# Gated delta rule round: three reorderings around the sixth level of the triangular inverse

## The chip, the cores and the metric

The program runs on one NeuronCore of a Trainium2 chip. The metric is the device time of one execution in microseconds; less is better. The engines are TensorE (PE), VectorE (DVE), ScalarE (ACT), GpSimd (POOL) and SyncE (SP, which here only starts weight loads). Each engine runs its own instruction stream in order and waits on semaphores.

## What is computed

Two blocks run one after the other on a sequence of 1024 tokens of width 1024, all in float32: a hybrid mixer (gated delta rule plus a convolution branch), cross attention over 256 memory rows and a gated feed-forward layer, and then a second block whose modulation is `silu(c) @ w_ada`. The change lies in the stage of the gated delta rule. The reference works in chunks; what matters is the unit triangular solve of each chunk and the recurrence over the chunks:

```
L = where(strict, einsum('id,jd->ij', kb, kc) * decay, 0)
sol = triangular_solve(eye + L, [v*beta, kb*exp(gc)])       # u, w
attn_intra = einsum('id,jd->ij', qc, kc) * decay
def step(S, ...):
    v_new = u_i - w_i @ S
    o = (q_i * exp(g_i)) @ S + a_i @ v_new
    S = S * exp(g_last) + k_dec.T @ v_new
# second block, independent of the first until its end:
mod = silu(c) @ w_ada + b_ada
```

## The kernel before

The sequence is cut into 8 tiles of 128 tokens; a tile holds 4 heads, side by side as 4 blocks of 128 columns. The stage `DeltaRule` is a software pipeline over rounds r = -1 to 9. In round r the engines prepare tile p = r+1 (`prep`), invert the triangle of tile i = r (`inv`) and carry the state for tile o = r-1 (`state`). The order in each round is written out by hand, once for each engine, in the methods `act`, `pe` and `dve`; semaphores (`after`, `prior`) tie them together.

The inverse is built in levels. The next tile's start, level 0, is: TensorE transposes the level-0 block `C0` (`ct`, L1667), VectorE makes `U` from it (`u0`, L1872), masks the level-1 block `C` (`c1`, `level_mask`, L1739) and copies `Tm` compactly to `Tc` (`x1`, `compact`, L1715). These three are "the next tile's triangle" here. Levels 1 to 6 are each: TensorE `y` (L1512, product of `U` and `C`), ScalarE copies it to `Y` (`copy_y`, L1475), TensorE `dd` (L1523, `d`, and up to level 5 also L1527, `t`), VectorE `update` (L1707 for `U`, L1710 for `Tm`, L1715). The sixth level is the last of a round: `y6`, its copy, `dd(i, 6)`, and `u6` on VectorE.

Other work shares the rounds. In even rounds 0 to 6 the convolution branch subtracts a mean (`cent`, L1854), in odd rounds 1 to 7 it makes a variance (`v_m`, L1858), and ScalarE raises it to the power -1/2 (L1440, L1442). GpSimd adds tiles for it in odd rounds (L1226, L1228). The state's output of tile o is scaled on VectorE: a small reduction (L1845 to L1061), ScalarE's `on_ln` and `on_y` (L1433, L1435), five small refinements (L1066 to L1862), the scaling `on` (L1865) and the product with the gate `og` (L1868). Once `og` is done ScalarE starts the load of a later gate into the freed buffer (`load_gate`, L1316), in rounds 1 to 6; instructions behind it on ScalarE wait until then.

The modulation of the second block has 12 weight strips, multiplied one strip at a time by `ada(j)` on TensorE (L1501) into a PSUM bank, from which `keep_ada` on ScalarE copies (L1326). Rounds 0 to 3 have two strips, rounds 4 to 7 one. The second strip of a round is the last item of TensorE's round, and its `keep_ada` stands on ScalarE behind `load_gate`. The next round begins on TensorE with transposes of q, k and v (`rows`, L1552) into the same banks, which wait for all strips kept; then `y1` (L1512), then column sums `ss` (L1562) of the squares `sq` that ScalarE makes as the first item of its round (L1366). VectorE begins its round's `prep` with `ss` (L1758). Then follow the transposes of the output (`oT`, L1574), which wait for the last state update `s3` (L1882), and `wT` (L1580), which waits for `u6`.

"The turn of round r" stands below for the stretch from `ct` of round r to `ss` of round r+1. After round 7 there is no next tile; TensorE goes on with the output product (L294), for which GpSimd splits weights (L3591, L3593).

Of the kernel before, what the change touches and what calls it, by code (L numbers as in the profile page):

```python
# [24 lines left out]
ALU = mybir.AluOpType  # L25
# [104 lines left out]
def after(eng, steps, name, rnd, back=0):  # L130

    eng.wait_ge(steps.sem, steps.at(name, rnd) - back * steps.n)


def prior(eng, steps, name, rnd):

    if rnd >= 0:
        after(eng, steps, name, rnd)


def build(nc, d, out):

    ctx = ExitStack()
    with ctx:
# [3 lines left out]
        def place(name, shape, dt=F32, at=None):  # L148

            at = top if at is None else at  # L150
            size = int(np.prod(shape[1:])) * 4
            t = nc.alloc_sbuf_tensor_at(name, shape, dt, offset=at["at"])
            at["at"] += (size + 63) // 64 * 64
            return t
# [7 lines left out]
        ident = place("ident", [P, P])  # L162
# [37 lines left out]
        def bank(b):  # L200
            return pp[b // 2][:, (b % 2) * 512:(b % 2) * 512 + 512]
# [28 lines left out]
        def mixed(x, l, pair=None):  # L230

            sz, whole = 1 << l, x[:, :, :]
            first, pairs = (0, 2) if pair is None else (pair, 1)
            return bass.AP(whole.tensor, whole.offset + first * P, [list(whole.ap[0]), [2 * sz, pairs * P // (2 * sz)], [2 * P + sz, 2], [1, sz]])

        def natural(x, l):

            return x.rearrange("p h (b two n) -> p (h b) two n", two=2, n=1 << l)
# [72 lines left out]
        class Stage:  # L311
# [25 lines left out]
            def act(self, act):  # L337
                pass
# [29 lines left out]
        class ResidualNorm:  # L368
# [31 lines left out]
            def load(self, act, t):  # L400
                s = t % self.slots
                act.dma_start(self.x[s][:, :], self.src[t * P:(t + 1) * P, :]).then_inc(norm_loaded[s], 16)
# [672 lines left out]
        class DeltaRule(Stage):  # L1075
# [233 lines left out]
            def act(self, act):  # L1309
# [46 lines left out]
                for r in range(-1, NT + 2):  # L1356
                    p, i, o = r + 1, r, r - 1
                    prep, inv, state = p < NT, 0 <= i < NT, 0 <= o < NT
                    f, fq = r % 2, r // 2
# [68 lines left out]
                        keep_ada(j)  # L1428
                    if 0 <= r < len(MEM_STRIPS):
                        self.keep_mem(act, r)  # L1430
                    if state:
                        after(act, self.ov, "on_m", o)
                        O_.done(act.activation(self.s4[:, 6, :], self.s4[:, 5, :], ACT.Ln), "on_ln")  # L1433
                        after(act, O_, "on_ln", o)
                        O_.done(act.activation(self.s4[:, 6, :], self.s4[:, 6, :], ACT.Exp, scale=-0.5), "on_y")  # L1435
                    if o == NT - 1:
                        branch(1, ("hi",))
                    if f == 1 and 0 <= fq < 4:
# [1 line left out]
                        F.done(act.activation(self.cr[1][:, :], self.cr[0][:, :], ACT.Ln), "v_ln")  # L1440
                        after(act, F, "v_ln", fq)
                        F.done(act.activation(self.cr[1][:, :], self.cr[1][:, :], ACT.Exp, scale=-0.5), "v_y")  # L1442
                    if inv:
                        self.copy_y(act, i, 6)
                    if prep and p + 2 < NT:
                        after(act, self.ps, "kq", p)
# [30 lines left out]
            def pe(self, pe):  # L1477
                PP, I, O = self.ps, self.is_, self.os
                def gates(*us):
                    for u in us if p == 0 else ():  # L1480
                        self.src.gate_unit(pe, u)
# [9 lines left out]
                def ada(j):  # L1491
                    strip = FIRST_STRIP[f"ada{j}"]
                    if j:
                        pe.wait_ge(self.ada_kept, j)
                    if prep:
                        after(pe, self.pv, "l3", p)
                    for half in range(2):
                        pe.wait_ge(w_loaded[half], (RAW_AT[strip] // 2 + 1) * 16)
                        for part in range(ADA_PARTS):
                            k = half * ADA_PARTS + part  # L1500
                            last = pe.matmul(bank(self.K_)[part * 32:part * 32 + 32, 0:SC], ada_c[:, k:k + 1].broadcast_to((P, 32)),  # L1501
                                             w_raw[:, k * SC:(k + 1) * SC], start=(half == 0), stop=(half == 1))
                        last.then_inc(w_ready, 1)
# [11 lines left out]
                def dd(i, l):  # L1515
                    after(pe, self.ia, f"y{l}", i)
                    if l == 1:
                        prior(pe, self.iv, "u6", i - 1)
                        after(pe, self.pv, "x1", i)
                    else:  # L1520
                        after(pe, self.iv, f"x{l}", i)
                    for pair in range(2):
                        last = pe.matmul(bank(self.B_)[:, pair * P:(pair + 1) * P], self.Tc[i % 2][:, pair, :], self.Y[:, pair, :], start=True, stop=True)  # L1523
                    I.done(last, f"d{l}")
                    if l < LEVELS - 1:
                        for pair in range(2):
                            last = pe.matmul(bank(self.A_)[:, pair * P:(pair + 1) * P], self.Y[:, pair, :], self.Tc[i % 2][:, pair, :], start=True, stop=True)  # L1527
                        I.done(last, f"t{l}")

                for r in range(-1, NT + 2):  # L1530
                    p, i, o = r + 1, r, r - 1
                    prep, inv, state = p < NT, 0 <= i < NT, 0 <= o < NT
                    f, fq = r % 2, r // 2
                    jobs = list(self.ada_of(r))
# [128 lines left out]
                    if prep:  # L1663
                        after(pe, self.pv, "c0", p)
                        after(pe, self.pa, "egb", p)
                        for pair in range(2):
                            last = pe.transpose(bank(self.G_)[:, pair * P:(pair + 1) * P], self.C0[:, pair, :], ident[:, :])  # L1667
                        PP.done(last, "ct")
                        gates(*range(11, 16))
                    if inv:  # L1670
                        dd(i, 6)
                    for j in jobs[1:]:
                        ada(j)

            def dve(self, dve):
                PV, IV, OV, F = self.pv, self.iv, self.ov, self.fv
                sm, al, tt = self.sm, self.al, dve.tensor_tensor
# [13 lines left out]
                def scal(x):  # L1691
                    return x.rearrange("p (h a) -> p h a", a=1).broadcast_to((P, GH, P))
# [21 lines left out]
                def compact(i, l):  # L1714
                    (IV if l > 1 else PV).done(dve.tensor_copy(natural(self.Tc[i % 2][:, :, :], l), mixed(self.Tm[i % 2], l)), f"x{l}")  # L1715
# [18 lines left out]
                def level_mask(i, l):  # L1734
                    if l > 2:
                        after(dve, self.is_, f"y{l - 2}", i)
                    else:
                        prior(dve, self.is_, f"y{l + 4}", i - 1)
                    (IV if l > 1 else PV).done(tt(self.masked(l, self.C[l % 2][:, :, :]), self.mixed(self.L[i % 2], l), self.masks(l, low_masks[:, l, :]), ALU.mult), f"c{l}")  # L1739

                for r in range(-1, NT + 2):
                    p, i, o = r + 1, r, r - 1
                    prep, inv, state = p < NT, 0 <= i < NT, 0 <= o < NT
                    f, fq = r % 2, r // 2
# [111 lines left out]
                    if f == 1 and 0 <= fq < 4:  # L1856
                        after(dve, self.fs, "sumsq", fq)
                        F.done(dve.tensor_scalar(self.cr[0][:, :], bank(self.F_)[:, 256:512], 1.0 / CW, EPS, ALU.mult, ALU.add), "v_m")  # L1858
                    if state:
                        recip_sqrt_refine(dve, self.oa, OV, "on", o, s4[:, 5, :], s4[:, 6, :], s4[:, 7, :])  # L1860
                        after(dve, OV, "on_r", o)
                        OV.done(tt(s4[:, 6, :], s4[:, 6, :], sc[:, o, RQ, :], ALU.mult), "oy")  # L1862
                        after(dve, OV, "oy", o)
                        prior(dve, self.os, "oT", o - 1)
                        OV.done(tt(self.on[:, :, :], b4(self.O2), scal(s4[:, 6, :]), ALU.mult), "on")  # L1865
                        after(dve, OV, "on", o)
                        skipped = ("s0", "s1", "s2", "s3") if o == NT - 1 else ()
                        OV.done(tt(self.on[:, :, :], self.on[:, :, :], self.gate[o % 2][:, :, :], ALU.mult), "og", *skipped)  # L1868
                    if prep:
                        after(dve, self.ps, "ct", p)  # L1870
                        after(dve, self.pa, "ui", p)
                        PV.done(tt(self.mixed(self.U[p % 2], 0), self.masks(0, ident[:, :]), self.masked(0, self.two(self.G_)), ALU.subtract), "u0")  # L1872
                        level_mask(p, 1)
                        after(dve, PV, "t0", p)
                        prior(dve, self.is_, "d6", p - 2)
                        compact(p, 1)
                    if inv:
                        update(i, 6)
                    if state and o < NT - 1:
# [1872 lines left out]
```

## Time and profile before

| | us |
|---|---|
| median of 3 runs | 2740.36 |
| lowest, highest | 2728.75, 2741.19 |
| the profiled execution | 2739.87 |
| its span | 2737.9 |

In the span TensorE is busy for 2618.3 us (96%), VectorE for 1660.1 us (61%), GpSimd for 1137.8 us (42%) and ScalarE for 835.1 us (31%). The rounds in which the change acts (r = 0 to 7) take from about 324 to 597 us of the span. A row of a timeline gives start, duration, engine, line, operation and tiles, and in brackets the idle time of the engine before it and who ended it. A matmul row that covers several instructions overlaps the next row by a pipeline's length, so starts are compared, not ends.

### The profile page before, as it was taken

To read this page: it belongs to the slowest core of one execution; us is meant where nothing else is said; L and a number is where in the kernel's file an instruction comes from. 1 tells how busy PE (TensorE), PEld (TensorE's weight loads), DVE (VectorE), ACT (ScalarE), POOL (GpSimd) and SP (SyncE) were. 2 spreads that over 40 slices of the span, in tenths; PEclk is the share of its full clock that TensorE was granted. 3 is DMA by queue.
4 is the path that set the end of the run, shared out by engine and by line. 5 is a ranking of instruction groups with operands and counts; after the bars stand their busy time and mean duration, and the time that the engine had idled before them with its cause. 6 is when DMAs were issued, how large, how long until landed. Compare 5 with 4: busy or idle time off the path is not lost.

```text
span 2737.9 us, 33162 instructions
## 1 busy us (share of the span) xinstructions
PE 2618.3 (96%) x13218; PEld 2183.8 (80%) x13218; DVE 1660.1 (61%) x2208; ACT 835.1 (31%) x1318; POOL 1137.8 (42%) x659
## 2 busy tenths in 40 slices
PE   6999988888999999999999998999999999999998
PEld 5788777877788877888888887788788888888887
DVE  4879967775503488666674467714365555487466
ACT  3011233323313333333333435311222222243342
POOL 2333100036740637777764454564211321142364
PEclk9999999999999999999999999999999999999999
DMA  4122233235321412222245453563433343465682
GB/s 150 61 86 93 96 120 124 81 103 184 123 74 62 151 66 77 85 77 85 77 141 194 159 184 108 200 209 129 138 108 108 108 135 120 139 254 206 227 312 108
DMA packets 147381, 360.25 MB, mean 132 GB/s; under 512 B 15173, under 2 KB 51229, under 8 KB 147100
## 3 DMA queue, kind: packets, MB, share of 16 engines
q1 hardware_dynamic: 65072, 177.81, 19.6%
q10 hardware_dynamic: 82156, 180.33, 18.5%
q8 instruction: 105, 1.72, 0.3%
q14 instruction: 48, 0.39, 0.0%
HBM read 268.90 MB, written 89.19 MB: 131 GB/s over the span
## 4 chain that ended last, share of the span: by engine, by line
PE 84%; DVE 9%; ACT 2%; POOL 2%; issue 1%; DMA 1%; ACTq 1%; DVEq 0%; POOLq 0%
PE pp L294 31%; PE pp L2171 13%; PE pp L2224 9%; PE pp L276 8%; PE pp L492 8%; PE pp L2894 2%; PE pp L1249 2%; POOL w_lo L3593 1%; PE pp L1935 1%; PE pp L1914 1%; DVE hgin_b L2700 1%; PE pp L1562 1%; PE pp L1523 1%; PE pp L442 1%; PE pp L2914 1%
## 5 line engine op out<-in xcount | busy, mean ns | idle before, releaser
L3591 POOL CAST w_hi<-w_raw 128x1024 fp32r<-128x1024 f32 x192 | 231.1, 1204 | 1058.9 <-PE pp L294 694.2
L294 PE MATMUL pp<-w_hi,act_hi 128*128 128x512 f32 x1344 | 541.8, 403 | 13.0 <-POOL w_lo L3593 8.8
L294 PE MATMUL pp<-w_hi,act_lo 128*128 128x512 f32 x1344 | 528.6, 393 | 0.0
L294 PE MATMUL pp<-w_lo,act_hi 128*128 128x512 f32 x1344 | 525.8, 391 | 0.0
L3593 POOL TENSOR_TENSOR w_lo<-w_raw,w_hi 128x1024 fp32r<-128x1024 f32 x192 | 487.4, 2539 | 15.4
L294 PEld LDWEIGHTS pp<-w_hi,act_hi 128*128 128x128 f32 x1344 | 254.0, 189 | 68.9 <-POOL w_lo L3593 10.1
L294 PEld LDWEIGHTS pp<-w_hi,act_lo 128*128 128x128 f32 x1344 | 253.2, 188 | 58.3
L294 PEld LDWEIGHTS pp<-w_lo,act_hi 128*128 128x128 f32 x1344 | 254.2, 189 | 51.4
L492 PE MATMUL pp<-act_hi,w_hi 128*128 128x512 f32 x480 | 192.5, 401 | 16.9 <-DVE act_lo L829 6.5
L492 PE MATMUL pp<-act_hi,w_lo 128*128 128x512 f32 x480 | 190.2, 396 | 0.0
L492 PE MATMUL pp<-act_lo,w_hi 128*128 128x512 f32 x480 | 190.0, 396 | 0.0
L2142 POOL TENSOR_TENSOR w_lo<-w_raw,w_hi 128x1024 fp32r<-128x1024 f32 x44 | 112.8, 2563 | 125.7 <-ACT w_hi L2136 125.7
L1025 DVE SCALAR_TENSOR_TENSOR mixin_conv<-pp,mixin_cw,mixin_conv 128x1023 f32<-128x1023 f32 (+14 forms) x120 | 152.0, 1266 | 3.6
L2490 DVE TENSOR_TENSOR ffn_gl<-ffn_graw,ffn_gh 128x512 fp32r<-128x512 f32 x44 | 88.0, 2011 | 80.4 <-ACT ffn_gh L2303 80.4
L2745 ACT ACTIVATE hg_st<-pp 128x512 f32<-128x512 f32 x104 | 61.7, 595 | 220.6 <-PE pp L294 183.9
L492 PEld LDWEIGHTS pp<-act_hi,w_hi 128*128 128x128 f32 x480 | 92.3, 192 | 38.8 <-issue 8.2
L2126 POOL TENSOR_TENSOR w_lo<-ffn_S,w_hi 128x512 fp32r<-128x512 f32 x76 | 116.3, 1552 | 7.3 <-ACT w_hi L2104 3.8
L3014 DVE COPY_PREDICATED hg_both<-up_masks,pp 128x512 f32<-128x512 int32 x56 | 41.2, 735 | 117.3 <-issue 117.2
L2224 PE MATMUL pp<-w_hi,ffn_gh 128*128 128x512 f32 x352 | 108.5, 390 | 0.0
L2224 PE MATMUL pp<-w_lo,ffn_gh 128*128 128x512 f32 x352 | 108.4, 389 | 0.0
L2224 PE MATMUL pp<-w_hi,ffn_gl 128*128 128x512 f32 x352 | 108.4, 389 | 0.0
L492 PEld LDWEIGHTS pp<-act_hi,w_lo 128*128 128x128 f32 x480 | 91.8, 191 | 19.9
(468 smaller groups left out, 5292.9 us busy)
## 6 DMA issues: line engine op xcount, KB each, us to landing
w_raw<-in_weights SPq DMA_DIRECT2D x314, 512.0 KB, 3.5
z_s<-hg_st ACTq DMA_DIRECT2D x52, 512.0 KB, 3.9
hid_s<-ffn_cb ACTq DMA_DIRECT2D x22, 512.0 KB, 2.6
ffn_graw<-hid_s ACTq DMA_DIRECT2D x44, 256.0 KB, 3.3
hg_qkb<-hT_s SPq DMA_DIRECT2D x16, 512.0 KB, 8.2
qkvT_s<-mixin_o ACTq DMA_DIRECT2D x12, 512.0 KB, 2.8
gdn_qkv<-qkvT_s ACTq DMA_DIRECT2D x8, 768.0 KB, 5.1
front_x<-in_x ACTq DMA_DIRECT2D x8, 512.0 KB, 5.3
```

What stands on the lines that cost most here:

```text
L276: last = pe.matmul(dst[:, h * hn:(h + 1) * hn], columns(w, j, k, mt * P, cols), a[:, k, h * hn:(h + 1) * hn], start=(k == 0 and w is w_hi ...
L294: last = pe.matmul(dst, a[:, k, t * P:(t + 1) * P], columns(w, j, k, 0, n), start=(k == 0 and a is high and w is w_hi), stop=(k == NK - 1 ...
L492: last = pe.matmul(dst, columns(w, j, k, mt * P, P), a[:, k, h * 512:(h + 1) * 512], start=(k == 0 and w is w_hi and a is act_hi), stop=(k ...
L1025: ins = dve.scalar_tensor_tensor(dst[:, j:T], pp[3][:, 0:T - j], w, dst[:, j:T], ALU.mult, ALU.add)
L2126: self.blocks.done(tt(self.four(self.block(w_lo, i, name)), self.source(name), self.four(self.block(w_hi, i, name)).bitcast(F32), ALU.subt ...
L2142: pool.tensor_tensor(w_lo[SLOT[q]][:, :], w_raw[:, r % 2 * HALF:(r % 2 + 1) * HALF], w_hi[SLOT[q]][:, :].bitcast(F32), ALU.subtract).then_ ...
L2171: last = pe.matmul(bank(dst), w[:, k * P:(k + 1) * P], a[:, k, :], start=(start and k == 0 and w is hi and a is acts[0]), stop=(stop and k ...
L2224: last = pe.matmul(pp[u][:, h * 512:(h + 1) * 512], g[a][:, u * P:(u + 1) * P], w[b][:, h * 512:(h + 1) * 512], start=(k == 0 and a == 0 a ...
L2490: self.gls.done(tt(self.piece(self.gl, n), self.piece(self.graw, n), self.piece(self.gh, n).bitcast(F32), ALU.subtract), "lo")
L2745: act.activation(self.st[s][:, row, :], self.dst(u), ACT.Copy).then_inc(self.kept, 1)
L3591: pool.tensor_copy(hi, raw).then_inc(w_split, 1)
L3593: pool.tensor_tensor(lo, raw, hi.bitcast(F32), ALU.subtract).then_inc(w_ready, 1)
```

## The change

Three pieces of the round are moved; no instruction is added or removed.

1. ScalarE: in odd rounds (f = 1) the copy of `y6` stands ahead of `on_ln`, `on_y` and the two steps of the variance. In even rounds it stays behind them.
2. TensorE: the second modulation strip of rounds 0 to 3 stands ahead of `dd(i, 6)`.
3. VectorE: the next tile's triangle (`u0`, `c1`, `x1`) stands ahead of the state's scaling (L1066 to `og`) instead of behind it.

```diff
@@ act
                     if 0 <= r < len(MEM_STRIPS):
                         self.keep_mem(act, r)
+                    if inv and f == 1:
+                        self.copy_y(act, i, 6)
                     if state:
                         after(act, self.ov, "on_m", o)
...
-                    if inv:
+                    if inv and f == 0:
                         self.copy_y(act, i, 6)
@@ pe
+                    for j in jobs[1:]:
+                        ada(j)
                     if inv:
                         dd(i, 6)
-                    for j in jobs[1:]:
-                        ada(j)
@@ dve
+                    if prep:
+                        after(dve, self.ps, "ct", p)
+                        after(dve, self.pa, "ui", p)
+                        PV.done(tt(self.mixed(self.U[p % 2], 0), ..., ALU.subtract), "u0")
+                        level_mask(p, 1)
+                        after(dve, PV, "t0", p)
+                        prior(dve, self.is_, "d6", p - 2)
+                        compact(p, 1)
                     if state:
                         recip_sqrt_refine(dve, self.oa, OV, "on", o, ...)
...
-                    if prep:
-                        (the same seven lines)
                     if inv:
                         update(i, 6)
```

On ScalarE, at the end of round 3, before (L1475 is the copy of `Y`, L1433 and L1435 are `on_ln` and `on_y`, L1440 and L1442 the variance, L1316 the gate's load, L1326 and L1328 the second strip's keep and store, L1366 the next round's squares):

```order
L1258 ACTIVATE kT<-pp 128x256 x2
L1433 ACTIVATE gdn_s_121<-gdn_s_121 128x4
L1435 ACTIVATE gdn_s_121<-gdn_s_121 128x4
L1440 ACTIVATE gdn_cr_157<-gdn_cr_156 128x256
L1442 ACTIVATE gdn_cr_157<-gdn_cr_157 128x256
L1475 ACTIVATE gdn_Y<-pp 128x256
L1313 DMA gdn_qkv_128<-qkvT_s 128x12x128
L1316 DMA gdn_gate_130<-gate_s 128x512
L1326 ACTIVATE gdn_row<-pp 128x256
L1328 DMA ada_s<-gdn_row 4x256
L1366 ACTIVATE gdn_sq<-gdn_qkv_129 128x1024
```

And now, where lines behind the inserted ones are numbered 2 higher:

```order
L1258 ACTIVATE kT<-pp 128x256 x2
L1477 ACTIVATE gdn_Y<-pp 128x256
L1435 ACTIVATE gdn_s_121<-gdn_s_121 128x4
L1437 ACTIVATE gdn_s_121<-gdn_s_121 128x4
L1442 ACTIVATE gdn_cr_157<-gdn_cr_156 128x256
L1444 ACTIVATE gdn_cr_157<-gdn_cr_157 128x256
L1313 DMA gdn_qkv_128<-qkvT_s 128x12x128
L1316 DMA gdn_gate_130<-gate_s 128x512
L1326 ACTIVATE gdn_row<-pp 128x256
```

The copy of `Y` moved past four instructions; the gate's load, the keep and the squares stand where they stood.

On TensorE, end of round 3 and begin of round 4, before (L1667 is `ct`, L1523 `dd(3, 6)`, L1501 the second strip, L1552 `rows`, L1562 `ss`):

```order
L1512 MATMUL pp<-gdn_U_152,gdn_C_168 128x128 x2
L1667 MATMUL pp<-ident,gdn_C_167 128x128 x2
L1523 MATMUL pp<-gdn_Y,gdn_Tc_153 128x128 x2
L1501 MATMUL pp<-w_raw,ada_c 32x256 x8
L1552 MATMUL pp<-ident,gdn_qkv_129 128x128 x8
L1512 MATMUL pp<-gdn_U_139,gdn_C_169 128x128 x2
L1562 MATMUL pp<-ones,gdn_sq 128x64 x8
```

And now:

```order
L1514 MATMUL pp<-gdn_U_152,gdn_C_168 128x128 x2
L1669 MATMUL pp<-ident,gdn_C_167 128x128 x2
L1503 MATMUL pp<-w_raw,ada_c 32x256 x8
L1525 MATMUL pp<-gdn_Y,gdn_Tc_153 128x128 x2
L1554 MATMUL pp<-ident,gdn_qkv_129 128x128 x8
L1514 MATMUL pp<-gdn_U_139,gdn_C_169 128x128 x2
L1564 MATMUL pp<-ones,gdn_sq 128x64 x8
```

The strip and `dd(3, 6)` changed places.

On VectorE, end of round 3, before (L1066 to L1868 are the state's scaling, L1872, L1739 and L1715 the next tile's triangle, L1707 is `u6`, L1882 the state update):

```order
L1858 TENSOR_SCALAR gdn_cr_156<-pp 128x256
L1066 TENSOR_TENSOR gdn_s_121<-gdn_s_121 128x4
L1068 TENSOR_TENSOR gdn_s_121<-gdn_s_121 128x4
L1070 TENSOR_SCALAR gdn_s_121<-gdn_s_121 128x4
L1072 TENSOR_TENSOR gdn_s_121<-gdn_s_121 128x4
L1862 TENSOR_TENSOR gdn_s_121<-gdn_s_121,gdn_sc 128x4
L1865 TENSOR_TENSOR gdn_on<-pp,gdn_s_121 128x512
L1868 TENSOR_TENSOR gdn_on<-gdn_on,gdn_gate_130 128x512
L1872 TENSOR_TENSOR gdn_U_139<-ident,pp 128x128x2
L1739 TENSOR_TENSOR gdn_C_169<-gdn_L_138,low_masks 128x256
L1715 COPY gdn_Tc_143<-gdn_Tm_165 128x256
L1707 TENSOR_TENSOR gdn_U_152<-gdn_U_152,pp 128x2x2x64
```

And now:

```order
L1860 TENSOR_SCALAR gdn_cr_156<-pp 128x256
L1864 TENSOR_TENSOR gdn_U_139<-ident,pp 128x128x2
L1741 TENSOR_TENSOR gdn_C_169<-gdn_L_138,low_masks 128x256
L1717 COPY gdn_Tc_143<-gdn_Tm_165 128x256
L1066 TENSOR_TENSOR gdn_s_121<-gdn_s_121 128x4
L1068 TENSOR_TENSOR gdn_s_121<-gdn_s_121 128x4
L1070 TENSOR_SCALAR gdn_s_121<-gdn_s_121 128x4
L1072 TENSOR_TENSOR gdn_s_121<-gdn_s_121 128x4
L1872 TENSOR_TENSOR gdn_s_121<-gdn_s_121,gdn_sc 128x4
L1875 TENSOR_TENSOR gdn_on<-pp,gdn_s_121 128x512
L1878 TENSOR_TENSOR gdn_on<-gdn_on,gdn_gate_130 128x512
L1709 TENSOR_TENSOR gdn_U_152<-gdn_U_152,pp 128x2x2x64
```

Three instructions moved past seven; `u6` and the state update stay where they were.

## Rows read from the trace of the kernel before

**Rows 1.** Waits, 310 to 610 us: who waited, for whom, us, times, longest
```profile
PE pp L1512 <- DVE gdn_C L1739: 5.7, 3, 3.0
```

**Rows 2.** Timeline of TensorE, turn of round 3: start, us, work, [idle before]
```profile
460.18 0.71 PE L1523 MATMUL pp<-gdn_Y,gdn_Tc 128*128 128x128 f32 x4 [2.15 <-ACT gdn_Y L1475]
460.82 1.51 PE L1501 MATMUL pp<-w_raw,ada_c 128*32 128x256 f32 x16
462.91 1.94 PE L1552 MATMUL pp<-ident,gdn_qkv 128*128 128x128 f32 x8 [0.57 <-ACT gdn_row L1326]
...
465.17 1.89 PE L1562 MATMUL pp<-ones,gdn_sq 128*128 128x64 f32 x16
```

**Rows 3.** Timeline of ScalarE, turn of round 3
```profile
461.57 0.33 ACTq L1316 DMA_DIRECT2D gdn_gate<-gate_s  x1
462.38 0.38 ACT L1326 ACTIVATE gdn_row<-pp 128x256 f32<-128x256 f32 x1 [2.25 <-PE pp L1501]
...
463.40 1.06 ACT L1366 ACTIVATE gdn_sq<-gdn_qkv 128x1024 f32<-128x1024 f32 x1 [0.63 <-ACT gdn_row L1326]
```

**Rows 4.** Timeline of VectorE, turn of round 3
```profile
458.88 0.41 DVE L1066 TENSOR_TENSOR gdn_s<-gdn_s 128x4 f32<-128x4 f32 x1
...
460.85 0.69 DVE L1868 TENSOR_TENSOR gdn_on<-gdn_on,gdn_gate 128x512 f32<-128x512 f32 x1
461.46 0.61 DVE L1872 TENSOR_TENSOR gdn_U<-ident,pp 128x256 f32<-128x256 f32 x1
...
462.43 0.41 DVE L1707 TENSOR_TENSOR gdn_U<-gdn_U,pp 128x256 f32<-128x256 f32 x1
```

**Rows 5.** Timeline of ScalarE and TensorE, turns of rounds 1 and 2
```profile
391.68 0.36 ACTq L1316 DMA_DIRECT2D gdn_gate<-gate_s  x1
393.44 0.38 ACT L1326 ACTIVATE gdn_row<-pp 128x256 f32<-128x256 f32 x1 [3.20 <-PE pp L1501]
...
427.92 0.34 ACTq L1316 DMA_DIRECT2D gdn_gate<-gate_s  x1
428.36 0.38 ACT L1326 ACTIVATE gdn_row<-pp 128x256 f32<-128x256 f32 x1 [3.39 <-DVE gdn_on L1868]
...
428.89 1.06 PE L1552 MATMUL pp<-ident,gdn_qkv 128*128 128x128 f32 x8 [2.16 <-DVE gdn_Tc L1715]
```

**Rows 6.** Timeline of ScalarE and TensorE, turn of round 4
```profile
497.00 1.06 ACT L1366 ACTIVATE gdn_sq<-gdn_qkv 128x1024 f32<-128x1024 f32 x1 [3.39 <-DVE gdn_on L1868]
...
497.36 0.75 PE L1512 MATMUL pp<-gdn_U,gdn_C 128*128 128x128 f32 x4 [2.11 <-DVE gdn_C L1739]
498.11 3.02 PE L1562 MATMUL pp<-ones,gdn_sq 128*128 128x64 f32 x16
```

**Rows 7.** Timeline of ScalarE and TensorE, turn of round 0
```profile
357.94 0.38 ACT L1326 ACTIVATE gdn_row<-pp 128x256 f32<-128x256 f32 x1 [1.83 <-PE pp L1501]
...
361.00 2.00 PE L1562 MATMUL pp<-ones,gdn_sq 128*128 128x64 f32 x16 [0.99 <-ACT gdn_sq L1366]
```

**Rows 8.** Timeline of TensorE, begin of round 7
```profile
567.85 1.11 PE L1574 MATMUL pp<-ident,gdn_on 128*128 128x128 f32 x4 [0.81 <-DVE gdn_S L1882]
```

**Rows 9.** Timeline of all engines, end of round 7 and begin of round 8
```profile
594.20 0.37 ACT L1475 ACTIVATE gdn_Y<-pp 128x256 f32<-128x256 f32 x1
...
594.36 2.21 DVE L1070 TENSOR_SCALAR gdn_s<-gdn_s 128x4 f32<-128x4 f32 x1
...
600.81 1.11 DVE L1882 SCALAR_TENSOR_TENSOR gdn_S<-gdn_S,gdn_sm,pp 128x128 f32<-128x128 f32 x4
...
594.19 2.35 POOL L3593 TENSOR_TENSOR w_lo<-w_raw,w_hi 128x1024 fp32r<-128x1024 f32 x1
...
602.26 0.60 PE L1574 MATMUL pp<-ident,gdn_on 128*128 128x128 f32 x4
```

**Rows 10.** Stretches: length, busy PE, PEld, DVE, ACT, POOL, granted clock, DMA share, GB/s
```profile
458.00:460.00 2.00, 0.03 (x1) 0.00 (x0) 1.86 (x7) 0.98 (x3) 1.20 (x2) 1.00 0.00 0
...
461.30:464.70 3.40, 2.83 (x21) 1.97 (x14) 2.92 (x10) 1.68 (x3) 0.00 (x0) 0.50 1.05 327
498.80:505.70 6.90, 6.90 (x34) 6.81 (x34) 2.28 (x7) 1.54 (x5) 0.00 (x0) 0.51 0.00 1
```

More of the change, by code:

```diff
@@ L1858, in dve @@
                         F.done(dve.tensor_scalar(self.cr[0][:, :], bank(self.F_)[:, 256:512], 1.0 / CW, EPS, ALU.mult, ALU.add), "v_m")
+                    if prep:
+                        after(dve, self.ps, "ct", p)
+                        after(dve, self.pa, "ui", p)
+                        PV.done(tt(self.mixed(self.U[p % 2], 0), self.masks(0, ident[:, :]), self.masked(0, self.two(self.G_)), ALU.subtract), "u0")
+                        level_mask(p, 1)
+                        after(dve, PV, "t0", p)
+                        prior(dve, self.is_, "d6", p - 2)
+                        compact(p, 1)
                     if state:
@@ L1868, in dve @@
                         OV.done(tt(self.on[:, :, :], self.on[:, :, :], self.gate[o % 2][:, :, :], ALU.mult), "og", *skipped)
-                    if prep:
[L1870 to L1876, printed above, removed]
                     if inv:
```

## The prediction, made before the result was known

> **What bounds the kernel now.** I read the waits between 310 and 610 us first, then the timelines of TensorE, ScalarE and VectorE side by side at each of the seven turns, and last the granted clock there. Inside a round TensorE hardly waits; it idles at the turns. The reader should see two kinds of wait. The one that catches the eye is what the change aims at: in the turn of round 3 `dd(3, 6)` waits 2.15 us for the copy of `Y` [rows 2] (round 1 reads the same, 2.15, round 5 2.10, round 7 1.24), and `y1` waits for the next tile's `C`, 5.7 us in three places [rows 1], one of them 2.11 us at the turn of round 4 [rows 6]. The other kind ends later. `ss` can't start before the squares `sq` exist, and `sq` is queued on ScalarE behind `load_gate`, which waits for `og` on VectorE. At the turn of round 4: `sq` waits for VectorE's `gdn_on` until 497.00, takes 1.06, ends at 498.06, and `ss` starts at 498.11 [rows 6]. `y1`, released at 497.36 by `C`, ended at about the same moment: two waits, and only the first is removed. At the turn of round 2 even `rows` hangs on it: the second strip's keep waits for `gdn_on` until 428.36 and `rows` starts at 428.89 [rows 5]. VectorE is busy through the whole turn (1.86 of 2.00 us [rows 10]), so what it does first decides who waits.
>
> **VectorE's piece.** Between the start of `u0` (461.46) and of `u6` (462.43) the three moved instructions take 0.97 us [rows 4]. They now stand ahead of the state's scaling, so `og` comes 0.97 us later in every round with state and a next tile, 1 to 6. In odd rounds a stall goes in return: L1066, a 128x4 operation that takes 0.16 us elsewhere, took 0.41 us at 458.88 [rows 4], beside GpSimd's addition, and its successors' spacing shows 0.25 us lost; `u0`, which takes its main input from PSUM, would stand there now. Odd rounds: 0.97 - 0.25 = 0.72 us. The Trainium skill ("SBUF — State Buffer", section "SBUF: two separate sides") says that a VectorE operation with two SBUF inputs is locked out while a GpSimd operation runs, and one whose input is PSUM is not; the 0.41 against 0.16 agrees, and without this rule the odd rounds would cost 0.97 too, 0.75 us more in all. `u6` and the state update keep their place in the queue, and total work ahead of them is the same, so `oT` and `wT` don't see the change in rounds 0 to 6.
>
> **TensorE's piece.** The strip takes about 1.07 us at full clock. It now fills the idle time in which `dd` waited for its copy. Its weights have landed: in 458 to 460 us nothing moves on the DMA queues [rows 10]. Its keep may follow sooner, but only if `load_gate` has gone. Once it starts, the keep can follow 0.44 us later, as in round 2, where nothing else held it (427.92 to 428.36 [rows 5]); in round 3 that is 461.57 to an earliest 462.01, though TensorE made the keep wait until 462.38 [rows 3].
>
> **ScalarE's piece.** The early copy removes the 2.15 us wait of `dd`, but nothing behind `dd` is in a hurry: `u6` is queued on VectorE until 462.43 [rows 4], and `rows` waits for the keep. `on_y` slips behind the copy to about 458.8; in rounds 1, 3, 5 the scaling now starts later than that, so no cost. Round 7 is different, below.
>
> **The sum, by turns.**
> - Round 0 (two strips, no state, so no `load_gate`): strip, keep and `sq` all come earlier by the place of `dd` and its wait, 357.94 to about 357.0, and `ss`, which waited 0.99 us for `sq` [rows 7], follows: -0.9.
> - Round 1: the keep stood at 393.44, waiting for TensorE [rows 5]. By the gate's load it can come at 391.68 + 0.44 + 0.72 = 392.84: -0.6.
> - Round 2: keep, `rows`, `sq`, `ss` all follow `og`: +0.97.
> - Round 3: 462.01 + 0.72 = 462.73 against 462.38: +0.35.
> - Round 4: `y1` 2.1 us earlier, but `ss` follows `sq`: +0.97.
> - Round 5: the same pattern as round 4 (`sq` at 532.88, `ss` at 533.99): +0.72.
> - Round 6: no tile is left to prepare in round 7, so no `sq`; `oT` waits for the state update until 567.85 [rows 8], which doesn't move: 0.
> - Round 7: no triangle to move, but the copy moves. It stood at 594.20 [rows 9]; `y6` ends near 593.4, so it starts there and pushes `on_y` from 592.5 to about 594.15. The refinements, which began at 593.31, begin at about 594.2, the moment at which GpSimd's L3593 starts at 594.19 for 2.35 us [rows 9]. L1070 there already lost 2.0 us to it. Now the first or second of four small steps is caught, and a later one by the next L3593 (597.61 to 600.01). I get `og` and `u6` some 2.1 us later, the state update from 600.81 to about 602.9, ending near 604.0. `oT` ran at 602.26 with the state done at 601.92, 0.34 us of slack [rows 9]: +1.8. Bounds: 0, if the steps fall in gaps, to +4.5, if L1868 also misses one and waits for the following split.
>
> Sum: -0.9 - 0.6 + 0.97 + 0.35 + 0.97 + 0.72 + 0 + 1.8 = **+3.3 us**.
>
> **The clock.** The granted clock falls to 0.50 (1.2 GHz) after some turns, and the work that follows runs at half speed: 3.4 us in 461.3 to 464.7 and 6.9 us in 498.8 to 505.7 [rows 10], also 6.4 us after round 1's idle and 6.9 after round 6's. After rounds 2 and 5, where TensorE idled about 2.1 us in one piece, it stayed at full. The change gathers each turn's idle time into one later piece, just ahead of dense work: in round 3 strip and `dd` end near 459.9 and `rows` starts near 463.3, 3.4 us against 2.15 and 0.57 before [rows 2]; in rounds 2, 4 and 5 I get 3.3 to 3.6. So I expect rounds 2 and 5 to lose the clock too. Half of a short low stretch is lost work: 1.7 us each (3.45 if they are long ones). I take the short ones: **+3.4 us**; bounds 0 and, with every turn long, +12.
>
> The profiled execution took 2739.87 us, 0.5 below the median of the three. 2739.87 + 3.3 + 3.4 = 2746.6, at the median **2747 us**.
>
> **Rivals.**
> *The visible waits were the bound (faster).* If `sq` were not held by `og` (if VectorE's work behind `v_m` ran faster, or `ss` could wait), four copies' waits of at most 2.15 and the 5.7 us of `C` [rows 1, 2] would go: -14.3, 2726 us. Against it stands the row at 497.00, in which `sq` names `gdn_on` [rows 6]. 6%.
> *The clock decides (slower).* Every one of the seven turns is followed by a long low stretch: 7 x 6.9 = 48.3 us against 6.4 + 3.4 + 6.9 + 6.9 = 23.6 now, half of the difference is 12.3, with the 3.3 above +15.6: 2755.5 us. It decides from the point at which an idle piece of 3.3 us always costs the clock and the recovery is never short. The Trainium skill ("TensorE: Matmul & The Clock Gate", "HAM oscillation — how this bites in real kernels") describes such a loop, in which a wait at every iteration throttles each one. For it: idle pieces of 2.1 us in rounds 1, 3 and 4 were enough. Against it: rounds 2 and 5, and the short recovery at 464.7 [rows 10]. 12%.
> *Nothing but the queue (little).* The clock keeps its four low stretches and round 7's steps fall in gaps: -0.9 - 0.6 + 3.0 = +1.5, 2741.9 us. 22%.
> That the moves don't take place can be left out; the order shows them.
>
> **How the numbers follow.** The forecast has 60%. I can tell no change from one within 0.5%, 13.7 us. The forecast and the third rival lie inside; the second rival straddles its edge (2754), the first lies at it (2727). So: faster 0.03, same 0.88, slower 0.09. The range goes from below the third rival by what separate executions differ (2728.75 was one of three before) to the second rival: 2734 to 2757.
>
> **What would show it.** Right: at the turns of rounds 1, 3, 5 `dd` without a wait for the copy; `y1` without a wait for `C`; instead `ss` waiting for `sq`, and `sq` or the keep naming `gdn_on`, about 1 us later counted from `v_m` or `cent`; longer unbroken idle of TensorE before `rows` or `ss`; low clock after rounds 2 and 5; in round 7 L1066 starting after 594 and `oT` waiting for the state. Wrong: `ss` starting at once behind `y1` at the turn of round 4, or the distance from `ct` to `ss` shrinking by 2 us there; then the first rival holds and my reading of who is last fails.

## The result, and the profile after

| | before | changed |
|---|---|---|
| median | 2735.95 us (20 runs) | 2745.09 us (20 runs) |
| lowest, highest | 2724.95, 2743.60 | 2735.43, 2750.15 |
| profiled execution, its span | 2739.87, 2737.9 | 2748.91, 2746.9 |
| ratio | 1 | 1.0034, 95% interval 1.0024 to 1.0043 |

The change costs about 9 us, 0.34%. The forecast had 2747 us, 6.7 more than the profiled execution of before; the two profiled executions differ by 9.0. TensorE is busy for 5.4 us more with the same instructions, 2623.7 us now against 2618.3. Three executions below, one each of three kernels, took 3372, 5425 and 9631 us; the ratios and means leave them out.

The waits between 310 and 610 us of the changed kernel (who waited, for whom: us in total, times, longest us) read as follows.

```profile
PEld pp L1564 <- ACT gdn_sq L1366: 11.1, 4, 3.5
...
PE pp L1564 <- ACT gdn_sq L1366: 10.3, 4, 3.3
...
ACT gdn_row L1326 <- DVE gdn_on L1878: 10.1, 3, 4.4
PE pp L1554 <- ACT gdn_row L1326: 9.8, 3, 3.5
...
ACT gdn_sq L1366 <- DVE gdn_on L1878: 7.2, 2, 4.4
```

Lines of the changed kernel are numbered 2 higher, or more inside what moved: L1554 is `rows`, L1564 `ss`, L1878 `og`. TensorE's wait for `C` [rows 1] is no longer a main wait, and `dd` no longer waits 2.15 us for its copy. In their place `ss` waits 10.3 us for the squares and `rows` 9.8 us for the keep, and the keep three times and the squares twice name `gdn_on` of VectorE as their own releaser. The wait that was removed had another behind it, and that one grew.

The timeline of TensorE at the turn of round 3 answers to [rows 2].

```profile
462.35 0.38 PE L1669 MATMUL pp<-ident,gdn_C 128*128 128x128 f32 x2
462.66 1.13 PE L1503 MATMUL pp<-w_raw,ada_c 128*32 128x256 f32 x16
463.72 0.71 PE L1525 MATMUL pp<-gdn_Y,gdn_Tc 128*128 128x128 f32 x4
467.96 1.94 PE L1554 MATMUL pp<-ident,gdn_qkv 128*128 128x128 f32 x8 [3.53 <-ACT gdn_row L1326]
...
470.55 3.51 PE L1564 MATMUL pp<-ones,gdn_sq 128*128 128x64 f32 x16
```

Strip and `dd` now run at once behind `ct`, without a wait. Then TensorE idles 3.53 us in one piece. Before it idled 2.15 and 0.57. The last row takes 3.51 us for the same 16 instructions that took 1.89: half clock.

On VectorE and ScalarE the same turn answers to [rows 3, 4].

```profile
463.58 0.61 DVE L1864 TENSOR_TENSOR gdn_U<-ident,pp 128x256 f32<-128x256 f32 x1
...
464.56 0.15 DVE L1066 TENSOR_TENSOR gdn_s<-gdn_s 128x4 f32<-128x4 f32 x1
...
466.28 0.69 DVE L1878 TENSOR_TENSOR gdn_on<-gdn_on,gdn_gate 128x512 f32<-128x512 f32 x1
466.89 0.41 DVE L1709 TENSOR_TENSOR gdn_U<-gdn_U,pp 128x256 f32<-128x256 f32 x1
```

```profile
467.00 0.33 ACTq L1316 DMA_DIRECT2D gdn_gate<-gate_s  x1
467.44 0.38 ACT L1326 ACTIVATE gdn_row<-pp 128x256 f32<-128x256 f32 x1 [2.87 <-DVE gdn_on L1878]
...
468.45 1.06 ACT L1366 ACTIVATE gdn_sq<-gdn_qkv 128x1024 f32<-128x1024 f32 x1 [0.63 <-ACT gdn_row L1326]
```

`u0` now starts at 463.58 in the place of L1066 and isn't held. L1066 takes 0.15 us instead of 0.41. `og` ends at 466.97, 4.62 us behind `ct`; before it ended at 461.54, 3.89 behind (`ct` at 457.65): 0.73 later. The keep no longer waits for TensorE, which finished the strip 3 us earlier, but for `gdn_on`.

The granted clock in four stretches of the changed kernel (columns as in [rows 10], clock third from the right):

```profile
391.50:402.00 10.50, 8.52 (x41) 8.55 (x42) 3.69 (x11) 2.94 (x5) 0.00 (x0) 0.52 0.48 160
467.10:477.40 10.30, 9.44 (x46) 9.47 (x47) 2.76 (x9) 3.65 (x8) 0.00 (x0) 0.51 0.37 123
507.60:514.50 6.90, 6.83 (x33) 6.83 (x34) 1.39 (x4) 2.15 (x7) 0.00 (x0) 0.53 0.07 22
432.70:436.10 3.40, 3.40 (x20) 3.40 (x18) 0.31 (x1) 1.96 (x3) 0.00 (x0) 0.52 0.51 200
```

After the turns of rounds 1 to 6 the changed kernel has low stretches of about 10.2, 3.4, 10.2, 6.8, 3.4 and 3.4 us. The kernel before had 6.8, none, 3.4, 6.8, none and 6.8.

**Turn by turn.** From the start of `ct` to the start of `ss` (us), with the change that the prediction gave:

| turn of round | before | changed | difference | predicted |
|---|---|---|---|---|
| 0 | 5.48 | 4.76 | -0.72 | -0.9 |
| 1 | 8.75 | 8.23 | -0.52 | -0.6 |
| 2 | 6.11 | 7.56 | +1.45 | +0.97 |
| 3 | 7.52 | 8.20 | +0.68 | +0.35 |
| 4 | 5.08 | 6.06 | +0.98 | +0.97 |
| 5 | 5.41 | 6.15 | +0.74 | +0.72 |
| 6 (`ct` to `oT`) | 5.89 | 5.89 | 0 | 0 |

The six turns add up to +2.6. The stretches between them, from `ss` to the next `ct`, hold the same work in both kernels and yet take 8.5 us more in the changed one (176.6 against 168.1, six rounds). The round after turn 1 took 27.86 us before and 30.76 now, that after turn 3 27.86 and 31.06: those are the rounds behind the 10 us low stretches. The rest of the program gives 2 us back in these two profiles; between 660 and 1500 us the kernel before has 10.2 us of low clock and the changed one none, so part of that is the clock too.

### The profile page after: what moved, and what is told of

Its sections match the earlier page's. It is cut to its first block, busy times and chain, and to the rows that moved or that the text cites. A ratio compares the mean times of both kernels' runs of the same rounds, so it can differ in the third digit from the quotient of the medians.

```text
span 2746.9 us, 33162 instructions
## 1 busy us (share of the span) xinstructions
PE 2623.7 (96%) x13218; PEld 2191.5 (80%) x13218; DVE 1668.3 (61%) x2208; ACT 834.8 (30%) x1318; POOL 1139.3 (41%) x659
## 4 chain that ended last, share of the span: by engine, by line
PE 83%; DVE 9%; ACT 2%; issue 2%; DMA 2%; POOL 2%; ACTq 1%; DVEq 0%; POOLq 0%
PE pp L294 31%; PE pp L2173 13%; PE pp L2226 9%; PE pp L276 8%; PE pp L492 8%; PE pp L2896 2%; PE pp L1249 2%; POOL w_lo L3595 1%; PE pp L1937 1%; PE pp L1916 1%; PE pp L1564 1%; DVE hgin_b L2702 1%; PE pp L2916 1%; PE pp L442 1%; PE pp L2917 1%
```

## Experiments

All ratios are to the kernel before, timed in the same session on the same chip. The experiments ran in three sessions on three chips, so two experiments are compared by their ratios, and such a difference is good to about 0.2%, 5 us. Turns and low stretches are read from one profiled execution of each.

### The three pieces apart

The change without its VectorE piece:

```diff
+                    if inv and f == 1:
+                        self.copy_y(act, i, 6)
...
+                    for j in jobs[1:]:
+                        ada(j)
                     if inv:
                         dd(i, 6)
-                    for j in jobs[1:]:
-                        ada(j)
```

> The change without its VectorE piece (copy of y6 and second strip moved, triangle where it was). If the delay of the gate's product on VectorE, passed on by the queued gate load on ScalarE, is the cause, it goes: the turns of rounds 2, 4 and 5 cost nothing, rounds 1 and 3 gain up to 1.3 and 0.4 us, round 0 gains 0.9, round 7 loses up to 1.8; together -1 to 0 us before the clock, so 0.999 to 1.001 of the kernel before. If instead the strip ahead of dd(6) is what costs (TensorE's idle time gathered into one later piece), the loss stays: 1.002 to 1.004.

Measured: 2738.44 us, ratio 1.0000 (0.9986 to 1.0015). The loss is gone. So the strip and the copy don't make it by themselves.

The VectorE piece alone:

```diff
+                    if prep:
+                        after(dve, self.ps, "ct", p)
...
+                        compact(p, 1)
                     if state:
                         recip_sqrt_refine(dve, self.oa, OV, "on", o, ...)
...
-                    if prep:
-                        (the same seven lines)
```

> The VectorE piece alone. Queue theory: +0.97 in the turns of rounds 2 and 4, +0.72 in round 5, +0.35 in round 3, 0 in rounds 0, 1, 6, 7, so +3.0 us, and more where the later work then meets the low clock: 1.001 to 1.003, with ss or the keep naming the gate's product. Rival, by which the earlier C is worth its visible waits: up to 5.7 us less, 0.998.

Measured: 2743.47 us, ratio 1.0022 (1.0007 to 1.0036), where all three pieces have 1.0034. The turns of rounds 2, 4 and 5 read 7.55, 6.07 and 6.13 us, as in the changed kernel. Turn 3 doesn't show the expected +0.35: it read 7.16 us against 7.52, without the low stretch that the kernel before has there. The profile is of the fastest of the 12 executions. The wait for `gdn_on` is there as forecast; this is the waits' view of it:

```profile
PE pp L1562 <- ACT gdn_sq L1366: 7.6, 4, 3.3
ACT gdn_sq L1366 <- DVE gdn_on L1876: 7.0, 2, 4.4
ACT gdn_row L1326 <- DVE gdn_on L1876: 7.0, 2, 4.4
```

The ScalarE piece alone:

```diff
+                    if inv and f == 1:
+                        self.copy_y(act, i, 6)
...
-                    if inv:
+                    if inv and f == 0:
                         self.copy_y(act, i, 6)
```

> The ScalarE piece alone: in odd rounds dd(6) starts 2.1 us earlier, and its strip with it. Queue theory: the keep of round 1 comes up to 1.3 us earlier (392.12 by the gate load against 393.44), of round 3 by 0.4; round 7 loses up to 1.8 by the late on_y; nothing elsewhere: -1.7 to 0, 0.999 to 1.001. Rival (visible waits): 2.15 us less in each of four rounds, 0.997.

Measured: 2732.25 us, ratio 0.9977 (0.9965 to 0.9988). This is more than I expected of it. Turn 1 took 6.54 us against 8.75, turn 3 6.48 against 7.52; 2, 4 and 5 are unchanged (6.10, 5.08, 5.42). That is 3.3 us less in rounds 1 and 3 (2.21 and 1.04), and nothing in round 5, where there is no second strip. Its profile has no low stretch behind turns 1 and 3, where the kernel before has 6.8 and 3.4 us, and that is all of the 3.3. In the last experiment of "Is it the clock?" the copy stands where it stood before, its wait is filled with throw-away matmuls, `dd` starts as late as ever, 2.55 us behind `ct` (2.52 before), and yet the turns of rounds 1 and 3 read 6.54 and 6.49 us. Its TensorE at turn 1 (the 9 throw-away matmuls are the 18 rows on `ident`):

```profile
387.45 0.38 PE L1670 MATMUL pp<-ident,gdn_C 128*128 128x128 f32 x2
387.67 2.17 PE L1677 MATMUL pp<-ident 128*128 128x128 f32 x18
390.00 0.71 PE L1523 MATMUL pp<-gdn_Y,gdn_Tc 128*128 128x128 f32 x4 [0.16 <-ACT gdn_Y L1475]
...
392.39 1.06 PE L1552 MATMUL pp<-ident,gdn_qkv 128*128 128x128 f32 x8 [0.68 <-DVE gdn_Tc L1725]
```

So the visible wait costs nothing as a wait; what it costs is the clock behind it.

The TensorE piece alone:

```diff
+                    for j in jobs[1:]:
+                        ada(j)
                     if inv:
                         dd(i, 6)
-                    for j in jobs[1:]:
-                        ada(j)
```

> The TensorE piece alone: the strip fills the wait of dd(6) for its copy. Queue theory: round 0 gains 0.9, round 1 up to 1.3, round 3 0.4, round 2 0, together -2.6 to -1: 0.999 to 1.000. If the strip ahead of dd(6) costs: over 1.001.

Measured: 2734.15 us, ratio 0.9992 (0.9978 to 1.0005), no change that can be told. Turns 0, 1 and 3 shrink by 0.7, 1.2 and 1.0 us, but the rounds after turns 1 and 5 took 31.05 and 31.80 us in its profile, with 10 us of low clock in each. The two pieces together (1.0000) are no better than either, which the turns don't explain: their sum is 34.7 us against 35.1 for the copy alone, and both have the same rounds between (168.3). The intervals of 1.0000 and 0.9977 just meet. Nor do the three pieces add up: alone they give -0.23, -0.08 and +0.22%, together +0.34. The mean granted clock of all executions (table under "Is it the clock?") differs in the same way: the copy alone has more of it than the kernel before, the strip alone and the two together have not. So the gain of the copy is one of the clock, and it is lost again when another piece moves; why the strip undoes it, these runs don't show.

### Is it the queued gate load?

All three pieces, with the gate's load moved out of the way of the keep and the squares, into the next round behind `nwT`:

```diff
-                    if state and o + 2 < NT:
-                        after(act, self.ov, "og", o)
-                        load_gate(o + 2)
                     for j in self.ada_of(r)[1:]:
                         keep_ada(j)
...
+                        if o and o + 1 < NT:
+                            after(act, self.ov, "og", o - 1)
+                            load_gate(o + 1)
```

> All three pieces, and the gate's load moved on ScalarE from ahead of the second strip's keep and of the next squares to behind nwT of the next round (it loads the same data, later). Queue theory: sq and the keep no longer wait for VectorE, ss starts right behind y1, each of the turns of rounds 1 to 5 loses its idle piece of 3 us, limited by VectorE, whose own idle before the next round's first step is 1 to 4 us now: 8 to 15 us less than the changed kernel, 0.995 to 0.999 of the kernel before. Rival, by which the gate load is not what holds the turn: no difference to the changed kernel, 1.003.

Measured: 2720.59 us, ratio 0.9941 (0.9920 to 0.9962). That is 25 us below the changed kernel, where 8 to 15 were expected, from a load that does the same work a little later. By the mean granted clock (table below) up to 14 us of it are half clock that went with the idle pieces. The turns of rounds 1 to 5 shrink to 4.50, 3.57, 4.45, 2.63 and 3.18 us. TensorE's timeline at the turn of round 4:

```profile
485.86 1.04 PE L1554 MATMUL pp<-ident,gdn_qkv 128*128 128x128 f32 x8
486.73 0.73 PE L1514 MATMUL pp<-gdn_U,gdn_C 128*128 128x128 f32 x4
487.30 1.89 PE L1564 MATMUL pp<-ones,gdn_sq 128*128 128x64 f32 x16
490.59 0.66 PE L1576 MATMUL pp<-ident,gdn_on 128*128 128x128 f32 x4 [1.40 <-DVE gdn_S L1884]
```

`ss` follows `y1` without a wait [rows 6 for before]. What is late next is the state update on VectorE, for which `oT` now waits 1.40 us.

The same move in the kernel before, with none of the three pieces:

> The kernel before (none of the three pieces), with the gate's load moved behind the next round's nwT as in the run with all three pieces that took 0.994. If the held squares are the main wait in both orders, most of that gain comes here too; but now the visible waits come last: dd(6) for its copy, 2.15 us in three turns, and y1 for C, up to 2.1 and 0.6. I expect 0.996 to 0.999, that is 5 to 10 us above the run with the three pieces. Rival, by which the three pieces are worth nothing once the load is late: the same 0.994.

Measured: 2733.00 us, ratio 0.9980 (0.9965 to 0.9995). In the order of before the late load is worth 0.2%, in the changed order 0.9% (1.0034 to 0.9941): without the three pieces, `dd` waits 2.1 to 2.2 us for the copy in turns 1, 3 and 5 (8.75, 6.46 and 5.69 us) and `y1` 2.11 us for `C` in turn 4 (5.13).

Copy and strip moved and the load late, the triangle where it was:

> Copy and strip moved and the gate load late, the triangle where it was. If moving the triangle is a gain once ss no longer waits for the gate's product, this stands above 0.9941: y1 waits for C again (2 us at the turns of rounds 4 and 5, 1 to 2 at those of 1 to 3), so 5 to 9 us more, 0.996 to 0.9975. If the triangle's place never mattered: 0.994.

Measured: 2727.79 us, ratio 0.9959 (0.9941 to 0.9977). Turns 2 to 5 read 4.91, 5.34, 5.11 and 5.27 us against 3.57, 4.45, 2.63 and 3.18 with the triangle moved. So the same VectorE piece costs 0.2% while `og` holds the squares, and once it doesn't, it gains: 7 to 8 us by the medians (2727.79 against 2720.59 and 2720.02), 5 to 7 by the ratios (0.9959 against 0.9941 and 0.9932, whose intervals overlap), 7.7 by the sum of turns 0 to 5 (30.8 against 23.1).

### Is it the clock?

The changed kernel with throw-away matmuls in the waits, which shorten no wait:

```diff
                     if inv:
                         dd(i, 6)
+                    if 1 <= r <= 3:
+                        for n in range(10):
+                            pe.matmul(bank(self.A_)[:, 256:384], ident[:, :], ident[:, :], start=True, stop=True)
...
+                    if 5 <= r <= 6:
+                        prior(pe, self.pv, "u0", p - 1)
+                        for n in range(10):
+                            pe.matmul(bank(self.G_)[:, 0:128], ident[:, :], ident[:, :], start=True, stop=True)
                     if prep:
                         after(pe, self.pa, "sq", p)
```

> All three pieces, plus 10 throw-away 128x128 matmuls on TensorE in the waits of the turns of rounds 1 to 5 (ahead of rows in rounds 1 to 3, ahead of ss in 4 and 5; about 0.22 us each, 2.2 us of the 2.8 to 3.5 idle). No wait is removed. Clock theory: the low stretches after these turns (some 34 us at 0.50 in the changed kernel's profile, of which about 12 us of time) disappear, and the kernel takes 6 to 12 us less than the changed one, 0.999 to 1.001 of the kernel before. If the queue alone made the difference, nothing changes: 1.003.

Measured: 2728.00 us, ratio 0.9970 (0.9955 to 0.9984), 17 us below the changed kernel by the medians, where 6 to 12 were expected. `ss` still waits for `gdn_on` as before; but where the changed kernel ran 6.9 us at half clock behind turn 4, this one has the following (columns as above, clock 1.00):

```profile
499.10:506.00 6.90, 6.90 (x55) 6.69 (x56) 3.79 (x17) 2.25 (x7) 0.00 (x0) 1.00 0.08 29
```

It shows 55 matmul rows in 6.90 us where the changed kernel shows 33.

The kernel before with 9 such matmuls ahead of `dd` in rounds 1, 3 and 5, of `rows` after round 2 and of `y1` after round 4:

> The kernel before with 9 throw-away 128x128 matmuls (about 0.22 us each) in its own waits: ahead of dd(6) in rounds 1, 3 and 5, ahead of rows after round 2, ahead of y1 after round 4. Clock theory: its low stretches after rounds 1, 3 and 4 (6.8, 3.4 and 6.8 us at 0.50) go, 4 to 8 us less, 0.997 to 0.9985; and the changed kernel with its throw-away matmuls (0.997) then stands 3 us, the queue's share, above it or level. If the clock played no part before: 1.000.

Measured: 2724.07 us, ratio 0.9940 (0.9925 to 0.9954). The direction is as expected, the size isn't: turns and rounds 1 to 6 explain 5.5 us of it (206.4 to 200.9), the medians differ by 14. In this profile the low stretches between 660 and 1500 us are missing too, where the code is the same.

With the clock held at full at the turns of rounds 1 to 5, the changed kernel's turns differ from the kernel before's by -0.82, +0.75, +0.97, +0.70, +0.98 and +0.74 us, in sum +3.3. That is the queue. From `ct` of round 0 to `ct` of round 6 the throw-away work took 12.5 us off the changed kernel (217.6 to 205.1) and 5.5 off the kernel before (206.4 to 200.9): 7.0 more of the time at half clock in this set of profiles. The two that are left differ by 4.2 us there, since the changed one still has a low stretch behind turn 0.

One profile is one execution, and the clock differs between executions of one kernel. The mean granted clock is on record for every execution of the changed kernels and for 75 of the kernel before, those of the three sessions. One minus that clock, times the span, is half of the time spent at half clock, and so the most that half clock can have cost:

| kernel | executions | mean granted clock | half of the time at half clock, us |
|---|---|---|---|
| before | 75 | 0.9868 | 36.2 |
| changed | 20 | 0.9854 | 40.2 |
| changed, round 7's copy back (below) | 11 | 0.9840 | 43.9 |
| strip and copy | 12 | 0.9869 | 35.8 |
| VectorE piece alone | 12 | 0.9854 | 40.0 |
| copy alone | 12 | 0.9885 | 31.4 |
| strip alone | 12 | 0.9866 | 36.7 |
| changed, gate load late | 6 | 0.9905 | 25.8 |
| before, gate load late | 12 | 0.9866 | 36.6 |
| changed, throw-away matmuls | 11 | 0.9915 | 23.1 |
| before, throw-away matmuls | 6 | 0.9913 | 23.6 |

The standard error of the last column is about 1 us (0.4 in the first row). The table shows three things. The change costs 4 us of clock by its 20 executions, and nearly 8 by the 11 of the kernel that differs from it in round 7 only; the 7.0 of the profiles lies between. The copy alone gains 5.4 us of clock against its own session's kernel before (36.8), about all of its 0.23%. And the throw-away matmuls took 13 us off the kernel before, more than the 17 us of low stretches at its turns can give at half, so low clock went elsewhere in the program too.

What is left between the two kernels with throw-away matmuls, whose granted clocks are the same, should be the queue's share; the expectation had 3 us. Whole times don't give it sharply: the medians differ by 3.9 us, the ratios (0.9970 and 0.9940) by 8, give or take 6. The share of the queue is therefore shown by the turns (+3.3), and that of the clock is 4 to 8 us; the two fill the 9 us that were measured, but how they share them is no closer known than that.

### Round 7

```diff
-                    if inv and f == 1:
+                    if inv and f == 1 and r < 7:
                         self.copy_y(act, i, 6)
...
-                    if inv and f == 0:
+                    if inv and (f == 0 or r == 7):
                         self.copy_y(act, i, 6)
```

> The changed kernel with the copy of y6 back in its old place in round 7 only. The prediction priced its move there at +1.8 us (GpSimd's splits catching VectorE's refinements). If that holds, 1.8 us less than the changed kernel, 1.0027 of the kernel before, with oT of round 8 waiting for nothing in both. The traces so far speak against it: in four kernels with the early copy the state update ends 10.5 to 10.8 us after the sum of squares and oT comes at 11.3 to 11.5 without a wait, and two kernels without it have the same 11.4. Then: no difference, 1.0034.

Measured: 2747.74 us, ratio 1.0029 (1.0014 to 1.0044): no difference from the changed kernel can be told, though 1.8 us would be too small to see here. The profiles are sharper. In the six with the early copy in round 7 the state update ends 10.5 to 10.8 us after the start of the sum of squares, in the seven without 9.4 to 9.7, so the copy makes it 1 us later. But `oT` comes at 11.2 to 11.6 us without a wait in all of them except the kernel before's (10.0), with the early copy and without. And on top of the late gate load:

> All three pieces with the late gate load, and round 7's copy back. Against the same without that step (0.9941): 0 to 2 us less if round 7 counts, else the same.

Measured: 2720.02 us, ratio 0.9932 (0.9915 to 0.9950), against 0.9941: the same within their intervals. These two have the lowest medians of all: 0.6 to 0.7% below the kernel before, 0.9 to 1.0% below the changed one. By the ratio the kernel before with throw-away matmuls stands level with them (0.9940).

## Why the prediction was right, and where it wasn't

**What ends last at a turn.** Right. `ss` waits for `sq`, `sq` for the queued gate load, that for `og`; the late-load kernel shows it directly, and the rival of the visible waits falls. In rounds 1 and 3 the wait for the copy did cost time, but through the clock behind it (the copy alone, above).

**VectorE's 0.97 and 0.72 us.** Right to a few hundredths. At turns 4 and 5, where nothing else intrudes, the profiles say +0.98 and +0.74, and with full clock in both kernels +0.75, +0.97, +0.70, +0.98, +0.74 for rounds 1 to 5. The alternation of even and odd rounds came out, so the stall of L1066 beside GpSimd's addition did go in odd rounds: `u0` took 0.61 us at 463.58 beside it, the same as at 461.46 without it. By the Trainium skill ("SBUF — State Buffer", section "SBUF: two separate sides") it is a VectorE operation with two SBUF inputs that GpSimd can lock out; `u0` has one, its other comes from PSUM, and the trace agrees.

**Rounds 1 and 3.** The terms -0.6 and +0.35 met the profile (-0.52, +0.68), but for a reason that the working didn't give. I read 0.6 and 0.4 us of TensorE's lateness there as order of work. They were low clock in the kernel before: with the clock held, its keep is on time in both rounds, and the change costs +0.75 and +0.70 there as in every odd round. The reading that the strip's weights have always landed was that of round 3: in round 1 of the changed kernel the earlier strip waits 0.60 us for them, at no cost, since the keep waits for `gdn_on` anyway.

**Round 7.** The term +1.8 was wrong. Its mechanism took place in part: L1066 started only once `on_y` had come, and two of its successors were caught by GpSimd's split, L1068 at 604.92 and L1872 at 608.33 for 2.22 us:

```profile
604.72 0.16 DVE L1066 TENSOR_TENSOR gdn_s<-gdn_s 128x4 f32<-128x4 f32 x1 [0.77 <-ACT gdn_s L1437]
604.92 2.20 DVE L1068 TENSOR_TENSOR gdn_s<-gdn_s 128x4 f32<-128x4 f32 x1
...
612.26 1.12 DVE L1884 SCALAR_TENSOR_TENSOR gdn_S<-gdn_S,gdn_sm,pp 128x128 f32<-128x128 f32 x4
```

```profile
614.23 0.60 PE L1576 MATMUL pp<-ident,gdn_on 128*128 128x128 f32 x4
```

The state update ended 10.6 us after the sum of squares started (602.79), where it had been 9.7 before (601.92, from 592.24): 0.9 later, not 2.1, since in the kernel before two operations were caught as well (L1070 and L1868). And `oT` came at 11.4 us without a wait, since the output product ahead of it ran 3.4 us at half clock. The profile of every experiment has a low stretch in this place as well, with the early copy and without; that of the kernel before happened not to. The slack that I read, 0.34 us, was that of one execution.

**The clock.** The direction was right: rounds 2 and 5 lost it, and the idle pieces were 2.8, 3.5, 3.5, 3.3 and 3.0 us in the turns of rounds 1 to 5, where I had 3.3 to 3.6. The size is less certain. I priced two further low stretches at 1.7 us each, 3.4 in all, and took the length of the others as given. In the profiles it measured 7.0, since those after rounds 1 and 3 grew from 6.8 and 3.4 to 10.2 us: for that execution the choice of the short stretch as price was the step that failed. Over the 20 executions the clock's share is 4 us, give or take 2, and 3.4 is no error; over the 11 of its near twin it is nearly 8. Between the ends that I gave, 0 and 12, all of these lie near the middle.

**The sum.** +3.3 for the queue held (3.3 by the turns with full clock), but with -0.6 and +0.35 in it that should have been +0.75 and +0.70, and 1.8 that should have been 0. Errors of 1.7 and 1.8 us cancelled, and that is luck. The total of 6.7 against 9.1 leaves 2.4 us, and the interval of the ratio, 6.6 to 11.8 us, just reaches it; the clock is the term that can hold the difference, but that isn't shown. That 2747 us stands within 2 us of the measured 2745.09 is luck once more: the three executions of before that I added to had a median of 2740.36 us, the twenty have 2735.95.

**The slower rival** (every turn followed by a long low stretch) came halfway: each of the turns of rounds 1 to 6 was followed by low clock in the changed kernel, but not by a long stretch each time. The Trainium skill ("TensorE: Matmul & The Clock Gate", section "HAM oscillation — how this bites in real kernels") describes such a loop and names work kept contiguous as the cure. Here throw-away matmuls in the wait did it, 17 us for 50 small matmuls.

## What to carry to other kernels

When a wait is to be removed, look for what else ends at the same moment: here `C` came at 497.36 and the squares at 498.06, and only the second was the bound, through a DMA start queued on ScalarE behind a semaphore. A DMA start that waits for a late event belongs behind everything on its queue that others need soon; moving it was worth more than the three reorderings, and it turned the one that cost into a gain. A wait can cost nothing as a wait and still cost the clock behind it, so a removed wait has two prices, and the second is read from the granted clock of many executions, not from one profile. In the turns of rounds 0 to 6 of the 13 profiles, each of the 24 idle pieces of TensorE of 2.97 us or more was followed by a low stretch, and so were 17 of the 28 between 2.0 and 2.9 us; that is a count, and no limit was measured.

## What was unexpected of the hardware

- Ten throw-away matmuls in each of five turns took 17 us off the changed kernel, and nine in each of five 14 to 16 us off the kernel before, though they shorten no wait.
- Low stretches came in lengths of about 3.4, 6.8 and 10.2 us, and the length did not follow the idle piece: 10.2 us behind pieces of 2.82 and 3.53 us in the changed kernel, but 3.4 behind one of 3.45, and 10.2 behind one of 2.10 in the kernel before with the late load. I had reckoned with 3.4.
- With strip and copy moved alone, TensorE idled 2.89, 2.48 and 2.85 us in one piece in the turns of rounds 1 to 3 and kept full clock in all three, so that gathering idle time into one piece is not by itself what costs.
- A lone idle piece of 2.1 us cost the clock in rounds 1, 3 and 4 of the kernel before and not in 2 and 5; between 660 and 1500 us, where the code is the same, profiles have 0 to 10 us of low clock.
